# Seven-product groups in the MLP's second matrix product, strips and groups in turn, and one of four weight sums made by an accumulating DMA that GpSimd issues

## The chip, the cores and the metric

One core of one Trainium2 chip. The metric is the device time of one launch in microseconds; the median of the runs of the kernel before is 2650.49 us (three runs, 2650.14 to 2651.08).

## The reference, cut to what matters

Two transformer-like blocks run over 256 tokens of width 2048, in float32. The change lies in the MLP of the first one:

```
ff = square(relu(h @ mlp_w1 + mlp_b1))          # (256, 2048) @ (2048, 8192)
h  = layer_norm(ALPHA * h + ff @ mlp_w2 + mlp_b2)   # (256, 8192) @ (8192, 2048)
```

Ahead of it stand a mixer with recurrences and its layer norm, behind it a second block (attention, convolution, gated MLP), which the change leaves alone.

## The kernel before, in words

**Numbers in two parts.** Every float32 operand of a matmul is split into a high part (a rounded copy, made by ScalarE) and a low part (the value less its high part, made by VectorE). A product is the sum of high x high, high x low and low x high. Weights come from HBM in pieces of 128 x 1024 floats, four to a quad (q), one in each slot r of a ring of four. SP loads slot r of quad q (`quad`, L284) once the low part of quad q-1 in this slot is made; ScalarE makes the high part (`split`, L885) once the piece has landed and TensorE is through with the slot's piece of the quad before (pe_piece); VectorE makes the low part (`lo`, L1369) behind the same two conditions. TensorE waits for both (`piece_ready`, L363).

**The MLP by blocks.** `mlp` stands once on each engine (L652 TensorE, L1145 ScalarE, L1769 VectorE), for blocks i = 0 to 7 of 1024 hidden features. A block is two strips and then two pairs of output strips:
- `strip` (L370) makes 512 hidden features from `xx` with two quads, first the high (L395) then the low matmuls (L406), the first strip into the four banks of `GB` (ps_b), the second into `GA` (ps_a). At its end ScalarE copies half of the result to `half` (`halves`, L895), VectorE adds bias and both halves into `hid` (L1777, four instructions), frees the banks (strip_out), squares the positive part (L1783), and high and low parts go to `ff` (L904, L1397).
- `token_pieces` (L491) multiplies `ff`, token tile by token tile, with pieces of mlp_w2. A run is one k tile by 512 output columns; for each run and each of two token tiles t it issues three matmuls of 512 columns (L504 to L506), so 12 matmuls a piece. A pair (two output strips of 512 columns, 8 k tiles, two token tiles) is 32 products, 96 matmuls. `W2_BANKS` (L253) says which banks an output strip uses.
- VectorE adds a finished output strip from its banks to the sum `zt` in SBUF (`add_tokens`, L1755).

**Order.** The order of the work is written out by hand in each engine's program. In a block it is strip, strip, pair, pair, and each engine's waits follow from it. On VectorE the low parts of the next quads stand between the other work. While block 0's first pair runs, `turn_seed` and `keep_seed` (L642, L1141) put the residual `res` into `zt`. GpSimd has little to do: it scales `res` (L2080) before the MLP and sums squares (L2089 to L2094) in later stages. Quads 74 to 137 are the MLP's.

Of the kernel before, what the change touches and what calls it, by code (L numbers as in the profile page):

```python
# [86 lines left out]
def build(nc, x_in, prm_in, const_in, w8, w10, out):  # L87

    with ExitStack() as ctx:
# [19 lines left out]
        def in_turn(name, size, *phases):  # L109
# [4 lines left out]
        (series, _, b3), (hh,), (mx, x_res), (res, bconv, probs, probs_t, vt), (_, squares2) = in_turn(  # L114
# [4 lines left out]
            [("mx", [P, KT, 2 * S], F32R), ("x_res", [P, 2, SN, S], F32)],  # L119
            [("res", [P, KT, S], F32),  # L120
# [12 lines left out]
        (gates, aa, tt), (vv,), (zz,), (zt, stats), (bug, hsq, hnb, cqt, ckt, aqt), (x2,) = in_turn(  # L133
# [6 lines left out]
            [("zt", [P, 2, SN, 512], F32), ("stats", [P, 2, SN, 6], F32)],  # L140
# [3 lines left out]
        (uf, uu), (hid, _, rms), (bpad,), (bsq, bmean, bsdev, bpart) = in_turn(  # L144
            "region_u", 3 * SN * S,
            [("uf", [P, SN, S], F32), ("uu", [P, SN, 2 * S], F32R)],
            [("hid", [P, 2, SN, S], F32), ("gap", [P, 3 * S], F32),
# [4 lines left out]
        half = sb("half", [P, SN, S])  # L152
        prm = sb("prm", [P, NPARAM])
# [78 lines left out]
        gate_sum, gate_act = sem("gate_sum"), sem("gate_act")  # L232
        tile_done, tile_out = sem("tile_done"), sem("tile_out")
# [19 lines left out]
        W2_BANKS = (GB[:, 0:2, :], GB[:, 2:4, :], GA[:, 0:2, :], GA[:, 2:4, :])  # L253

# [28 lines left out]
        def _(sp):  # L283
# [54 lines left out]
            with sp.Fori(0, 68) as i:  # L338
                quad(i + 74, w8, 4 * i + 224, N8)
# [16 lines left out]
        def _(pe):  # L356
# [237 lines left out]
            def turn_normed(n, b):  # L594

                if b == 0:
                    pe.wait_ge(*((z_kept, 1) if n == 0 else (acc_out, 38)))
                if b == 1:
                    pe.wait_ge(*((z_kept, 5) if n == 0 else (acc_out, 40)))
# [42 lines left out]
            def turn_seed(b):  # L642
# [3 lines left out]
                for j in range(SN):  # L646
                    for t in range(2):
                        last = nc.tensor.transpose(W2_BANKS[2 + b % 2][:, t, j * P:j * P + P],
# [3 lines left out]
            def mlp(i, first=False):  # L652

                q, e = 8 * i + 74, 2 * i + E_MLP
                if first:
                    strip(q, e, GB, xx, KT, need_normed(0), free=lambda: pe.wait_ge(z_kept, 3), turns=False)
                    strip(q + 2, e + 1, GA, xx, KT, nothing)
                else:
                    strip(q, e, GB, xx, KT, nothing, free=lambda: pe.wait_ge(acc_out, 5 * i - 3), by_pairs=True)
                    strip(q + 2, e + 1, GA, xx, KT, nothing, free=lambda: pe.wait_ge(acc_out, 5 * i), by_pairs=True)  # L660
                for pair in (0, 2):
                    for c in range(2):
                        for n in (pair, pair + 1):
                            if c == 0:
                                pe.wait_ge(strip_out, outs(e + 1 + pair // 2))
                                if first and pair == 2:
                                    pe.wait_ge(seed_kept, n + 1)
                            pieces = [(q + 4 + pair + c, 2 * (n % 2) + h,
                                       [(4 * c + 2 * h, 0, 0, 512), (4 * c + 2 * h + 1, 0, 512, 512)]) for h in range(2)]
                            if n == 3 and c == 1:  # L670
                                token_pieces(pieces, W2_BANKS[n], ff, 8, need_ff(2 * i), z_half)
                                continue
                            for _, r, runs in pieces:
                                if first and pair == 0 and (c, r) in ((0, 2), (0, 3), (1, 1), (1, 2)):
                                    if (c, r) == (0, 2):
                                        pe.wait_ge(strip_out, outs(e + 2))
                                    turn_seed(((0, 2), (0, 3), (1, 1), (1, 2)).index((c, r)))
                                token_pieces([(q + 4 + pair + c, r, runs)], W2_BANKS[n], ff, 8, need_ff(2 * i))

            mlp(0, True)  # L680
            with pe.Fori(0, 7) as i:
                mlp(i + 1)

            pe.wait_ge(acc_out, 37)
# [20 lines left out]
            strip(138, E_IN2, GB, xx, KT, need_normed(1), free=lambda: pe.wait_ge(acc_out, 37), turns=False)  # L705
# [178 lines left out]
        def _(act):  # L884
# [256 lines left out]
            def keep_seed(b):  # L1141
                act.wait_ge(seed_turned, b + 1)
                act.activation(zt[:, :, b, :], W2_BANKS[2 + b % 2], ACT.Copy).then_inc(seed_kept, 1)

            def mlp(i, first=False, last=False):  # L1145
                q, e = 8 * i + 74, 2 * i + E_MLP
                for k in range(2):
                    if not (first and k == 0):
                        splits(q + 2 * k + 1)
                    splits(q + 2 * k + 2)  # L1150
                    halves(e + k, 4 * (q + 2 * k) + 8, psum[1 - k])
                    hi_of(ff[:, 4 * k:4 * k + 4, 0:S], hid[:, k, :, :], ff_made, 2 * i + k + 1, ff_hi)
                if first:
                    splits(q + 5, N8, (0, 1))
                    keep_seed(0)
                    split(q + 5, 2)
                    keep_seed(1)
                    split(q + 5, 3)
                    split(q + 6, 0)
                    keep_seed(2)  # L1160
                    split(q + 6, 1)
                    keep_seed(3)
                    splits(q + 6, N8, (2, 3))
                else:
                    splits(q + 5)
                    splits(q + 6)
                if last:
                    act.activation(warm[:, 1:2], eps[:, 0:1], ACT.Sqrt)
                splits(q + 7)
                splits(q + 8, N8, (0, 1) if last else range(RING))  # L1170

            mlp(0, True)
            with act.Fori(0, 6) as i:
                mlp(i + 1)
            mlp(7, last=True)
# [190 lines left out]
        def _(dve):  # L1366
# [388 lines left out]
            def add_tokens(i, q, n, t, count):  # L1755

                if isinstance(i, int) and i == 0:
                    dve.wait_ge(seed_kept, n + 1)
                else:
                    dve.wait_ge(acc_out, 5 * i - 4 + count)  # L1760
                if t == 0:
                    dve.wait_ge(z_half, i + 2)
                else:
                    dve.wait_ge(pe_piece, 4 * (q + 5 + n - n % 2) + 2 + 2 * (n % 2))
                blocks = slice(0, 2) if t is None else t
                dve.tensor_tensor(zt[:, blocks, n, :], W2_BANKS[n][:, blocks, :], zt[:, blocks, n, :], ALU.add
                                  ).then_inc(acc_out, 1)

            def mlp(i, first=False, last=False):  # L1769
                q, e = 8 * i + 74, 2 * i + E_MLP  # L1770
                for k in range(2):
                    if not (first and k == 0):
                        los(q + 2 * k + 1)
                    los(q + 2 * k + 2, N8, (0, 1, 2))
                    dve.wait_ge(half_out, e + k + 1)
                    for j in range(SN):
                        ins = dve.scalar_tensor_tensor(hid[:, k, j, :], psum[1 - k][:, j, 0:S],  # L1777
                                                       column("b1", 4 * k + j + 8 * i), half[:, j, :], ALU.add, ALU.add)
                    ins.then_inc(strip_out, 1)
                    lo(q + 2 * k + 2, 3)  # L1780
                    dve.wait_ge(strip_out, outs(e + k + 1))

                    dve.scalar_tensor_tensor(hid[:, k, :, :], hid[:, k, :, :], 0.0, hid[:, k, :, :], ALU.max,  # L1783
                                             ALU.mult).then_inc(ff_made, 1)
                    lo_of(ff[:, 4 * k:4 * k + 4, S:2 * S], hid[:, k, :, :], ff[:, 4 * k:4 * k + 4, 0:S],
                          2 * i + k + 1, ff_hi, ff_lo)

                def summed(n):
                    if last:
                        dve.wait_ge(acc_out, 36 + n)  # L1790
                        for t in range(2):
                            strip_stats(n, t, zt[:, t, n, :])

                los(q + 5)
# [416 lines left out]
```

## Time and profile before

| | us |
|---|---|
| median of three runs | 2650.49 |
| lowest, highest | 2650.14, 2651.08 |
| span of the profiled execution, first to last instruction | 2647.7 |
| TensorE busy | 2631.6 (99%) |
| VectorE busy | 1745.8 (66%) |
| ScalarE busy | 1362.4 (51%) |
| GpSimd busy | 36.1 (1%) |

The page gives the profiled execution's span; its own whole time is not printed apart from the three runs' times. A row of a timeline is a start, a length, the engine and what it did; "x4" says that four like instructions are merged in it, and brackets give the idle time ahead and what ended it. Consecutive instructions of one engine overlap a little: the length of one is a bit more than the distance of two starts. A matmul's length holds its way through the array; the pace is the distance of the starts. PE is TensorE, PEld its weight loads, DVE VectorE, ACT ScalarE, POOL GpSimd, SP the engine that issues the loads.

### The profile page before, as it was taken

How to read it: one execution, taken by the hardware profiler on the slowest of the kernel's cores; microseconds unless marked ns; L12 is line 12 of the kernel's file. 1: busy time of each engine (PE TensorE's matmuls, PEld its weight loads, DVE VectorE, ACT ScalarE, POOL GpSimd, SP SyncE). 2: the span in 40 equal slices, each digit the busy share in tenths (PEclk: the TensorE clock that was granted, in tenths of full speed). 3: DMA queues.
4: the chain of work that ended last, by engine and by line, in shares of the span. 5: the costliest groups of instructions: out<-in, count | busy, mean ns of one | idle time of the engine just before them, and what ended most of it. 6: DMA issues, size and time to landing. Idle time of an engine off the chain costs nothing.

```text
span 2647.7 us, 40522 instructions
## 1 busy us (share of the span) xinstructions
PE 2631.6 (99%) x14379; PEld 2279.8 (86%) x14379; DVE 1745.8 (66%) x1863; ACT 1362.4 (51%) x1588; POOL 36.1 (1%) x30
## 2 busy tenths in 40 slices
PE   9999999999999999999999999999999999999999
PEld 8888888888888888888888888878888888888888
DVE  7787877544455655555555568996666666666667
ACT  5767765444444544444444445587554444444444
POOL 0000000000000100000000001000100000000000
PEclk9999999999999999999999999999999999999999
DMA  7555555555656455556555664534555555555554
GB/s 266 181 186 184 191 186 195 197 182 189 201 198 199 160 187 193 176 192 202 192 178 193 198 195 153 177 129 147 171 191 190 188 186 188 190 190 190 190 190 168
DMA packets 133881, 494.01 MB, mean 187 GB/s; under 512 B 14864, under 2 KB 15376, under 8 KB 133776
## 3 DMA queue, kind: packets, MB, share of 16 engines
q1 hardware_dynamic: 133776, 492.62, 56.4%
q8 instruction: 65, 1.06, 0.2%
q14 instruction: 40, 0.33, 0.0%
HBM read 490.46 MB, written 2.10 MB: 186 GB/s over the span
## 4 chain that ended last, share of the span: by engine, by line
PE 92%; DVE 3%; ACT 2%; issue 2%; DMA 0%; DVEq 0%; SPq 0%; ACTq 0%
PE ps_b L395 18%; PE ps_a L395 18%; PE ps_b L406 10%; PE ps_a L406 10%; PE ps_b L504 6%; PE ps_b L506 6%; PE ps_b L505 6%; PE ps_a L505 5%; PE ps_a L504 5%; PE ps_a L506 5%; DVE w_lo L1373 1%; PE ps_b L826 1%; ACT w_hi L889 1%; DVE bconv L1874 1%; DVE gates L1519 1%
## 5 line engine op out<-in xcount | busy, mean ns | idle before, releaser
L1373 DVE TENSOR_TENSOR w_lo<-w_raw,w_hi 128x1024 fp32r<-128x1024 f32 (+1 forms) x908 | 1120.4, 1251 | 726.3 <-ACT w_hi L889 716.9
L889 ACT ACTIVATE w_hi<-w_raw 128x1024 fp32r<-128x1024 f32 (+1 forms) x908 | 966.9, 1075 | 1105.1 <-PE ps_a L506 237.1
L395 PE MATMUL ps_b<-xx,w_hi 128*128 128x512 f32 x1184 | 287.9, 392 | 4.0 <-DVE xx L1690 2.3
L395 PE MATMUL ps_a<-xx,w_hi 128*128 128x512 f32 x1120 | 269.1, 391 | 0.0
L395 PEld LDWEIGHTS ps_b<-xx,w_hi 128*128 128x128 f32 x1184 | 216.9, 188 | 47.7 <-ACT w_hi L889 3.7
L395 PEld LDWEIGHTS ps_a<-xx,w_hi 128*128 128x128 f32 x1120 | 205.8, 188 | 39.8
L395 PE MATMUL ps_a<-x,w_hi 128*128 128x512 f32 x704 | 165.9, 390 | 0.0
L395 PE MATMUL ps_b<-x,w_hi 128*128 128x512 f32 x704 | 165.5, 390 | 0.0
L406 PEld LDWEIGHTS ps_b<-xx,w_lo 128*128 128x128 f32 x1184 | 153.2, 192 | 5.8
L406 PE MATMUL ps_b<-xx,w_lo 128*128 128x256 f32 x1184 | 156.0, 284 | 0.0
L395 PEld LDWEIGHTS ps_b<-x,w_hi 128*128 128x128 f32 x704 | 130.8, 188 | 26.2
L395 PEld LDWEIGHTS ps_a<-x,w_hi 128*128 128x128 f32 x704 | 130.6, 188 | 26.1
L406 PEld LDWEIGHTS ps_a<-xx,w_lo 128*128 128x128 f32 x1120 | 142.3, 191 | 4.4
L406 PE MATMUL ps_a<-xx,w_lo 128*128 128x256 f32 x1120 | 144.4, 283 | 0.0
L504 PE MATMUL ps_b<-w_hi,xx 128*128 128x512 f32 (+1 forms) x320 | 122.6, 383 | 0.0
L506 PE MATMUL ps_b<-w_hi,xx 128*128 128x512 f32 (+1 forms) x320 | 121.3, 379 | 0.0
L505 PE MATMUL ps_b<-w_lo,xx 128*128 128x512 f32 (+1 forms) x320 | 121.3, 379 | 0.0
L504 PE MATMUL ps_b<-w_hi,ff 128*128 128x512 f32 x256 | 99.9, 390 | 0.0
L506 PE MATMUL ps_b<-w_hi,ff 128*128 128x512 f32 x256 | 99.6, 389 | 0.0
L505 PE MATMUL ps_b<-w_lo,ff 128*128 128x512 f32 x256 | 99.6, 389 | 0.0
L504 PE MATMUL ps_a<-w_hi,ff 128*128 128x512 f32 x256 | 99.6, 389 | 0.0
L505 PE MATMUL ps_a<-w_lo,ff 128*128 128x512 f32 x256 | 99.6, 389 | 0.0
(305 smaller groups left out, 3933.5 us busy)
## 6 DMA issues: line engine op xcount, KB each, us to landing
w_raw<-w_dram SPq DMA_DIRECT2D x836, 512.0 KB, 3.4
w_raw<-w_dram SPq DMA_DIRECT2D x72, 640.0 KB, 3.9
zz<-x_dram SPq DMA_DIRECT2D x8, 256.0 KB, 4.6
x_res<-x_dram SPq DMA_DIRECT2D x4, 512.0 KB, 6.0
out_dram<-res SPq DMA_DIRECT2D x3, 512.0 KB, 2.8
out_dram<-res SPq DMA_DIRECT2D x4, 128.0 KB, 2.1
const<-const_dram SPq DMA_DIRECT2D x1, 449.0 KB, 4.5
prm<-prm_dram SPq DMA_DIRECT2D x1, 308.0 KB, 5.4
```

What stands on the lines that cost most here:

```text
L395: last = nc.tensor.matmul(group[:, j, :], w_hi[:, r, o * P:o * P + P], moving(src, at + k), start=begins and k == 0, stop=not begins and k ...
L406: last = nc.tensor.matmul(group[:, j, 0:S], w_lo[:, r, o * P:o * P + P], moving(src, at + k)[:, 0:S], start=begins and k == 0, stop=not be ...
L504: nc.tensor.matmul(dst, x_hi, hi, start=k == 0 and not begun, stop=False)
L505: nc.tensor.matmul(dst, x_hi, lo, start=False, stop=False)
L506: last = nc.tensor.matmul(dst, x_lo, hi, start=False, stop=k == kt - 1)
L826: nc.tensor.matmul(banks[:, j // 2, (j % 2) * S:(j % 2) * S + S], w_hi[:, r, cols], mix_tile(k)[:, half_at:half_at + S], start=False, stop ...
L889: act.activation(w_hi[:, r, 0:width], w_raw[:, r, 0:width], ACT.Copy).then_inc(hi_done, 1)
L1373: dve.tensor_tensor(w_lo[:, r, 0:width], w_raw[:, r, 0:width], w_hi[:, r, 0:width].bitcast(F32), ALU.subtract).then_inc(lo_even if r % 2 = ...
L1519: own.done(dve.tensor_tensor_scan(gates[:, hd, way, 0, order], aa[:, way, hd, order], tt[:, way, hd, order], 0.0, ALU.mult, ALU.add))
L1874: ins = dve.scalar_tensor_tensor(y, x, column("cv_w", n), y, ALU.mult, ALU.add)
```

## The change

Blocks are taken apart and put in turn: strip, pair, strip, pair. All strips but the second use `GB`. The strip of a block's first half is made ahead of the second pair of the block before. In 13 of the 16 pairs (block 0's second, both of blocks 1 to 6) the 2 x 2 x 2 products of two token tiles, two k tiles and two output strips on k tiles 2 and 3, and again on 4 and 5, are made by seven products instead of eight (Winograd's form); k tiles 0, 1, 6 and 7 stay as they were. The seven need sums of inputs and of weights:
- four sums of `ff` tiles (`next_inputs_of`), once a block on VectorE, with their high and low parts in spare columns of the ring (`s_hi_of`, `s_lo_of`);
- four sums of weights. The one for m5 is made in the ring slot by a DMA from HBM that adds the other piece to what has landed (`added`, GpSimd), the other three by two VectorE subtractions from it (`mixed_pieces`). These three get high and low parts of 1536 columns (`t_high`, `t_low`); ScalarE and VectorE take the slot's own parts only after the DMA has landed (t1_in).
- Four of the products go to the four banks of `GB`, and VectorE adds them into `q_acc` in SBUF (two adds a pair, `group_end`), three with the plain products into `GA`, added to `zt` as before. `q_acc` is cleared by GpSimd and combined into `zt` by `combined`, five VectorE instructions for each of the two pairs, in and after block 6.

The last block writes to `ff_last` and runs in the old order of banks. SP's order of pieces within a grouped pair changes with it (`by_groups`).

```diff
+        def product_operands(g, wh, wl, r0, buf):
...
+            return dict(m1=(GB[:, 0, :], tile(k, 0), piece(r0, 0)),
+                        m2=(GA[:, 0, :], tile(k + 1, 0), piece(r0, 1)),
+                        m3=(GA[:, 2, :], summed(3), piece(r1, 1)),
+                        m4=(GA[:, 1, :], tile(k + 1, 1), mixed_piece(2)),
+                        m5=(GB[:, 1, :], summed(0), piece(r1, 0)),
+                        m6=(GB[:, 2, :], summed(1), mixed_piece(0)),
+                        m7=(GB[:, 3, :], summed(2), mixed_piece(1)))
...
+            def seven_products(i, g, done, q, r0):
+
+                m = product_operands(g, w_hi, w_lo, r0, g)
+                piece_ready(q, r0)
+                product(m["m1"], g == 0, g == 1)
+                product(m["m2"], False, False).then_inc(pe_piece, 1)
+                piece_ready(q, r0 + 1)
+                product(m["m5"], g == 0, g == 1)
+                product(m["m3"], False, False).then_inc(pe_piece, 1)
+                pe.wait_ge(t_hi, done + g + 1)
+                pe.wait_ge(t_lo, done + g + 1)
+                product(m["m6"], g == 0, g == 1)
+                last = product(m["m7"], g == 0, g == 1)
+                if g == 1:
+                    last.then_inc(q_out, 1)
+                product(m["m4"], False, False).then_inc(t_used, 1)
+
+            def grouped(i, pair, q):
...
+                for nn in range(2):
+                    pe.wait_ge(acc_out, 2 * n - 1 + nn)
+                    token_pieces([(q, nn, two_tiles(0))], sums_of(nn), ff, 8, need)
...
+                seven_products(i, 0, 2 * n - 2, q, 2)
+                need(4)
+                seven_products(i, 1, 2 * n - 2, q + 1, 0)
+                for nn in range(2):
+                    token_pieces([(q + 1, 2 + nn, two_tiles(6))], sums_of(nn), ff, 8, nothing)
...
+            def mlp(i):
+
+                q, e = 8 * i + 80, E_MLP + 2 * i + 3
+                grouped(i, 0, q)
+                up_strip(q + 2, e, lambda: pe.wait_ge(q_kept, 4 * i))
+                grouped(i, 1, q + 4)
...
+            def second_of(n, q, r0):
+
+                act.wait_ge(t1_in[1 - r0 // 2], 8 * n + 16 - 8 * (1 - r0 // 2))
+                split(q, r0 + 1)
...
+            def strip_end(q, e, k, sums, n):
+
+                splits(q + 2, N8, (0, 1, 2))
+                if sums is not None:
+                    act.wait_ge(s_lo, sums + 1)
+                halves(e, 4 * q + 8, GB)
+                second_of(n, q + 2, 2)
+                t_high(n, 0)
+
+            def group_end(q, n):
+
+                split_group(n + 1, q + 1, 0)
+                t_high(n + 1, 1)
+                splits(q + 1, N8, (2, 3))
+                splits(q + 2)
...
+            def mixed_pieces(n, q, r0, buf):
+
+                even, odd = w_raw[:, r0, 0:N8], w_raw[:, r0 + 1, 0:N8]
+                made = t_raw[:, buf, :]
+                dve.wait_ge(raw_in[r0], 16 * q + 16)
...
+                dve.wait_ge(t1_in[buf], 8 * n + 16 - 8 * buf)
+                own.done(dve.tensor_tensor(made[:, 0:512], odd[:, 0:512], odd[:, 512:N8], ALU.subtract))
+                own.need()
+                dve.tensor_tensor(made[:, 512:1536].rearrange("p (h c) -> p h c", h=2),
+                                  even.rearrange("p (h c) -> p h c", h=2),
+                                  made[:, 0:512].unsqueeze(1).to_broadcast([P, 2, 512]), ALU.subtract).then_inc(t_made, 1)
...
+            def strip_end(q, i, k, n):
+
+                e = E_MLP + 2 * i + k
+                los(q + 2, N8, (0, 1))
+                activated(e, i, k, GB)
+                squared(e + 1, k)
+                mixed_pieces(n, q + 2, 2, 0)
+                los(q + 2, N8, (2, 3))
+                t_low(n, 0)
+
+            def group_end(q, pair, n, done):
+
+                mixed_pieces(n + 1, q + 1, 0, 1)
+                los(q + 1, N8, (0, 1))
+                t_low(n + 1, 1)
+                los(q + 1, N8, (2, 3))
+                los(q + 2, N8, (0, 1))
+                dve.wait_ge(q_out, done + 1)
+                for h in range(2):
+                    dve.tensor_tensor(q_acc[:, pair, 2 * h:2 * h + 2, :], GB[:, 2 * h:2 * h + 2, :],
+                                      q_acc[:, pair, 2 * h:2 * h + 2, :], ALU.add).then_inc(q_kept, 1)
+                lo(q + 2, 2)
+                add_sums(pair, 0, 4 * q + 7)
+                lo(q + 2, 3)
+                add_sums(pair, 1, 4 * q + 8)
...
+            pool.wait_ge(seed_kept, 4)
+            pool.memset(q_acc[:, :, :, :], 0.0).then_inc(q_zero, 1)
+
+            def added(n, q, at, r0):
+
+                pool.wait_ge(raw_in[r0 + 1], 16 * q + 16)
+                pool.dma_start(w_raw[:, r0 + 1, 0:512], w8[ds(at, 1), :, 0:512].rearrange("a p n -> (a p) n"),
+                               accum_op=ALU.add).then_inc(t1_in[1 - r0 // 2], 16)
```

## Rows read from the trace of the kernel before

**Rows 1.** The page: engines' busy time, and the chain that ended last, by engine.
```profile
PE 2631.6 (99%) x14379; PEld 2279.8 (86%) x14379; DVE 1745.8 (66%) x1863; ACT 1362.4 (51%) x1588; POOL 36.1 (1%) x30
PE 92%; DVE 3%; ACT 2%; issue 2%; DMA 0%; DVEq 0%; SPq 0%; ACTq 0%
```

**Rows 2.** Busy time by windows, one MLP block: us, engines, granted clock, DMA share, GB/s.
```profile
1245.30:1333.40 88.10, 88.10 (x450) 75.53 (x449) 50.88 (x50) 37.05 (x36) 0.00 (x0) 1.00 0.58 191
```

**Rows 3.** Timeline of TensorE: two strips and the first pair of that block.
```profile
1245.30 3.79 PE L395 MATMUL ps_b<-xx,w_hi 128*128 128x512 f32 x16
...
1267.53 3.79 PE L395 MATMUL ps_a<-xx,w_hi 128*128 128x512 f32 x16
...
1289.76 0.39 PE L504 MATMUL ps_b<-w_hi,ff 128*128 128x512 f32 x1
...
1311.52 0.39 PE L504 MATMUL ps_a<-w_hi,ff 128*128 128x512 f32 x1
```

**Rows 4.** Groups of VectorE by line and form: busy us, mean ns, idle before.
```profile
L1373 DVE TENSOR_TENSOR w_lo<-w_raw,w_hi 128x1024 fp32r<-128x1024 f32 x836 | 1014.4, 1231 | 659.1 <-ACT w_hi L889 651.6 <-DVE hid L1385 3.4 <-DVE padded L1385 1.9
L1373 DVE TENSOR_TENSOR w_lo<-w_raw,w_hi 128x1280 fp32r<-128x1280 f32 x72 | 106.1, 1490 | 67.2 <-ACT w_hi L889 65.3 <-issue 1.7
...
L1842 DVE TENSOR_TENSOR hid<-hid,rms 128x1024 f32<-128x1024 f32 x22 | 26.8, 1219 | 0.0
...
L1766 DVE TENSOR_TENSOR zt<-ps_b,zt 128x1024 f32<-128x1024 f32 x16 | 19.6, 1224 | 6.7 <-PE ps_b L506 6.7
...
L1397 DVE TENSOR_TENSOR xx<-zz,xx 128x512 fp32r<-128x512 f32 x8 | 5.5, 686 | 2.6 <-ACT xx L908 2.6
```

**Rows 5.** Groups of ScalarE by line and form.
```profile
L889 ACT ACTIVATE w_hi<-w_raw 128x1024 fp32r<-128x1024 f32 x836 | 875.1, 1058 | 1006.9 <-PE ps_b L506 221.7 <-PE ps_a L506 184.1 <-PE ps_b L395 173.2
L889 ACT ACTIVATE w_hi<-w_raw 128x1280 fp32r<-128x1280 f32 x72 | 91.7, 1274 | 98.2 <-PE ps_a L506 52.9 <-PE ps_a L448 11.1 <-PE ps_b L448 9.3
```

**Rows 6.** Timelines of ScalarE and of VectorE behind the strip's end at 1267.53.
```profile
1267.79 1.06 ACT L889 ACTIVATE w_hi<-w_raw 128x1024 fp32r<-128x1024 f32 x1 [0.81 <-PE ps_b L395]
1268.75 1.01 ACT L900 ACTIVATE half<-ps_b 128x1024 f32<-128x1024 f32 x1
...
1269.90 1.66 DVE L1777 SCALAR_TENSOR_TENSOR hid<-ps_b,prm,half 128x256 f32<-128x256 f32 x4 [1.58 <-ACT half L900]
...
1276.10 3.50 DVE L1373 TENSOR_TENSOR w_lo<-w_raw,w_hi 128x1024 fp32r<-128x1024 f32 x3
```

**Rows 7.** Timelines: VectorE behind a wait on itself, TensorE behind one on VectorE.
```profile
1807.14 0.69 DVE L1938 TENSOR_TENSOR bpart<-bconv 128x512 f32<-128x512 f32 x1
1807.87 0.42 DVE L1940 TENSOR_TENSOR bpart<-bpart 128x256 f32<-128x256 f32 x1
...
1820.36 0.42 DVE L1940 TENSOR_TENSOR bpart<-bpart 128x256 f32<-128x256 f32 x1
...
1820.93 0.67 PE L626 MATMUL ps_a<-bpart,ones 128*128 128x256 f32 x2 [0.72 <-DVE bpart L1940]
```

**Rows 8.** The page: DMA issues, KB each, us from issue to landing.
```profile
w_raw<-w_dram SPq DMA_DIRECT2D x836, 512.0 KB, 3.4
...
zz<-x_dram SPq DMA_DIRECT2D x8, 256.0 KB, 4.6
...
out_dram<-res SPq DMA_DIRECT2D x4, 128.0 KB, 2.1
```

**Rows 9.** Timelines of GpSimd and VectorE where both work, in order of time.
```profile
903.34 3.69 DVE L1373 TENSOR_TENSOR w_lo<-w_raw,w_hi 128x1024 fp32r<-128x1024 f32 x3
903.52 12.24 POOL L2080 TENSOR_SCALAR res<-res,prm 128x256 f32<-128x256 f32 x16 [903.08 <-DVE xx L1687]
...
1625.71 9.59 POOL L2089 TENSOR_TENSOR squares<-squares 128x1024 f32<-128x1024 f32 x3 [709.95 <-ACT squares L1126]
1626.72 6.31 DVE L1373 TENSOR_TENSOR w_lo<-w_raw,w_hi 128x1024 fp32r<-128x1024 f32 x2 [0.38 <-ACT w_hi L889]
...
1874.33 2.61 POOL L2089 TENSOR_TENSOR squares<-squares 128x1024 f32<-128x1024 f32 x1 [235.08 <-ACT squares L1126]
```

**Rows 10.** Busy time by windows, where TensorE stands still now and then (columns as rows 2).
```profile
1820.00:1840.00 20.00, 18.11 (x156) 16.67 (x155) 13.74 (x21) 17.08 (x37) 0.00 (x0) 1.00 0.38 125
```

More of the change, by code:

```diff
@@ L647, in turn_seed @@
                     for t in range(2):
-                        last = nc.tensor.transpose(W2_BANKS[2 + b % 2][:, t, j * P:j * P + P],
+                        last = nc.tensor.transpose(W2_BANKS[b % 2][:, t, j * P:j * P + P],
                                                    res[:, SN * b + j, t * P:t * P + P], ident)
                 last.then_inc(seed_turned, 1)
[L652 to L678, printed above, removed]
@@ L680, in _, with two_tiles, up_strip, product @@
-            mlp(0, True)
-            with pe.Fori(0, 7) as i:
-                mlp(i + 1)
-            pe.wait_ge(acc_out, 37)
+            def two_tiles(k):
+                return [(k, 0, 0, 512), (k + 1, 0, 512, 512)]
+            def up_strip(q, e, free):
+                strip(q, e, GB, xx, KT, nothing, free=free, by_pairs=True)
+            def product(operands, begins, ends):
+                bank, (a_hi, a_lo), (b_hi, b_lo) = operands
+                nc.tensor.matmul(bank, a_hi, b_hi, start=begins, stop=False)
+                nc.tensor.matmul(bank, a_hi, b_lo, start=False, stop=False)
+                return nc.tensor.matmul(bank, a_lo, b_hi, start=False, stop=ends)
@@ new lines, in in_order @@
+            def in_order(q, banks, src, need, begin=None, beside=None, apart=None):
+                for c in range(2):
+                    for nn in range(2):
+                        if c == 0 and begin is not None:
+                            begin(nn)
+                        pieces = [(q + c, 2 * nn + h, two_tiles(4 * c + 2 * h)) for h in range(2)]
+                        if apart is not None and (c, nn) == (1, 1):
+                            token_pieces(pieces, banks(nn), src, 8, need, apart)
+                            continue
+                        for _, r, runs in pieces:
+                            if beside is not None:
+                                beside(c, r)
+                            token_pieces([(q + c, r, runs)], banks(nn), src, 8, need)
@@ L1753, in _, with add_tokens @@
             first_blocks(0, 74)
[L1755 to L1764, printed above, removed]
+            def add_tokens(n, banks, t, count):
@@ new lines, in next_inputs_of @@
+            def next_inputs_of(i, q):
+                dve.wait_ge(ff_made, 2 * i + 2)
+                h = pairs[:, 1:3, :, :, :]
+                one, two, three_, four = (s_sum[:, n, :, :] for n in range(4))
+                own.done(dve.tensor_tensor(one, h[:, :, 0, 1, :], h[:, :, 1, 1, :], ALU.add))
+                own.need()
+                own.done(dve.tensor_tensor(two, one, h[:, :, 0, 0, :], ALU.subtract))
+                own.need()
+                own.done(dve.tensor_tensor(three_, h[:, :, 0, 1, :], h[:, :, 0, 0, :], ALU.subtract))
+                dve.tensor_tensor(four, h[:, :, 1, 0, :], two, ALU.subtract).then_inc(s_made, 1)
+                ff_low(ff, i, 0)
+                lo(q + 1, 0)
+                ff_low(ff, i, 1)
+                lo(q + 1, 1)
+                lo_of(s_lo_of, half[:, :, :], s_hi_of, i + 1, s_hi, s_lo)
+                los(q + 1, N8, (2, 3))
```

350 lines of the change are left out of this document (258 added, 92 removed).

## The prediction, made before the changed kernel was run

> **What bounds the kernel now.** I read the page first: TensorE is busy 99% of the span, VectorE 66%, ScalarE 51%, GpSimd 1%, and the chain that ended last lies 92% on TensorE [rows 1]. Then one block of the MLP by windows: from 1245.30 to 1333.40 TensorE is busy for all 88.10 us, at full granted clock (2.4 GHz), VectorE 50.88 us and ScalarE 37.05 us [rows 2]. So the stage is matmul after matmul, and only fewer matmuls could shorten it, as long as the others keep up. Last the timelines, for the pace: a strip starts at 1245.30 and the next at 1267.53, so a strip costs 22.23 us; the 96 token products of a pair of output strips start at 1289.76 and the next pair at 1311.52, 21.76 us or 0.2267 us a matmul [rows 3]. A token piece of 12 matmuls is 2.72 us.
>
> **What the change removes.** In 13 groups (block 0's second pair, both pairs of blocks 1 to 6) the 16 products on k tiles 2 to 5 become 14. A product is three matmuls, so a pair falls from 96 matmuls to 90, 20.40 us, 1.36 us less. 13 x 1.36 = **-17.7 us**.
>
> **What it adds.** On TensorE nothing. On VectorE, per block of two strips and two pairs: four 512-wide subtractions (0.69 each), four 1024-wide ones with a broadcast input (1.22, the price of the broadcast product of L1842), four low parts of 1536 (1.75: 1.231 at 1024, 1.490 at 1280, so 0.26 more for 256 more), four more PSUM adds (1.22), and once four 256-wide sums (0.46, with a wait) and a low part (1.23) [rows 4, 7]. That is 2.8 + 4.9 + 7.0 + 4.9 + 1.8 + 1.2 = 22.6 us more on 50.9, so 73.5 of some 85 us. VectorE is not the bound by its total. What matters is where the work stands, because a ring slot is prepared only four pieces ahead. ScalarE gets four high parts of 1536 (1.49: 1.058 at 1024, 1.274 at 1280) and one of 1024 [rows 5], 7 us in all on 37; not a bound.
>
> **The walk through one group.** Count from E, the end of the strip ahead (E = 1267.53 in the block shown). TensorE's own course would be: plain pieces 0 and 1 of quad q until 5.44; products on slot 2 until 6.80, on slot 3 until 8.16, the three that need the mixed pieces until 10.20; the same for quad q+1 until 14.96; two plain pieces until 20.40. VectorE's course begins with the strip's end, which in the new order is always directly ahead of a group:
> - ScalarE is released 0.26 after E (1267.79) and VectorE starts on the strip 1.15 after the copy of the half (1268.75 to 1269.90) [rows 6]. The copy now goes ahead of the split of slot 3, so it starts at E+0.26 and VectorE at E+1.41.
> - Four additions take 1.66, until 3.07. A wait of VectorE on itself costs 0.04 (1807.14 + 0.69 to 1807.87) [rows 7]. The square starts at 3.11; without a wait the next instruction starts 1.14 later ((3.50 - 1.23)/2) [rows 6], at 4.25.
> - Mixed pieces: 0.69 + 0.04, then 1.22: ends 6.20. Slots 2 and 3 may be taken low only now (lows free the raw slots): 6.12 to 7.35, 7.26 to 8.49. ScalarE's high part of the mixed pieces runs beside, 6.23 to 7.72. The low part runs 8.40 to 10.15.
> - TensorE wanted slot 2 at 5.44. A wait of TensorE on VectorE ends 0.15 after the instruction (1820.36 + 0.42 to 1820.93) [rows 7], so it goes on at 7.50, is through slots 2 and 3 at 10.22, waits for the low part until 10.30 and ends the first seven at 12.34: 2.14 late.
> - Second seven: mixed pieces 10.06 to 12.01, lows of slots 0 and 1 until 13.16 and 14.30, low part of the mixed pieces 14.21 to 15.96. TensorE waits for slot 0 until 13.31, is at the mixed products at 16.03, gets them at 16.11, ends them at 18.15: **3.19 late**. The plain pieces at the end have their lows at 17.10 and 18.24, before they are due (18.15, 20.87).
>
> So from E+1.41 to E+15.96 VectorE has no gap, and TensorE needs that chain done at 12.77 (its own course to the mixed products of the second seven, 12.92, less 0.15). The stalls start afresh in each group, since the chain hangs on the strip's end. The group ends at 23.59 where 21.76 was before: +1.83, and 13 x 1.83 = **+23.8 us**.
>
> **What else is moved.** After a group VectorE takes two lows (until 20.4), the two adds out of the B banks (until 22.8, 0.8 before TensorE wants these banks for the next strip), two more lows and the two sums, until 3.7 after the group's end. In strips where the next inputs are made it is then busy until about 14.6 of the strip, while the strip's low matmuls on its second quad come at 14.8 to 17.6: covered, with 0.1 to 3 us to spare, and if that cover goes the strip waits by the excess. At the end combined(1) puts 5.2 us and a low part 1.2 us ahead of the lows of quad 135: these end at 11.4 where TensorE wants them at 10.9, **+0.6 us** with the release. The strips alternate through the B banks alone; their adds are out in time as said, so nothing for that. SP's ring loads are freed by the lows: the latest (slot 3, next-inputs strip) is issued at E-7.6.
>
> **The accumulating DMA** has no row. It waits for the raw piece: an issue at E-7.6 with 3.4 us to landing [rows 8] gives E-4.2 (elsewhere E-5.1). VectorE wants the sum at 4.25, so 8.45 us are free; the second one has from E+0.6 to 10.06, 9.4 us. Ends: 2.1 us (a 128 KB transfer) and 9.2 us (twice the 4.6 of a 256 KB load, since the destination is read as well) [rows 8]. At 9.2 it is 0.75 us late, x 13 = +9.8 us. I take nothing, from the single 4.6 us load, the nearest in size. Queued behind it: on ScalarE the split of slot 3 and then the high part of the mixed pieces, on VectorE the whole chain, on GpSimd the next issue; its sums of squares, first at 1625.71 [rows 9], come long after. By the Trainium skill, "DMA: Bandwidth & Descriptors", section on the anatomy of one DMA, such a transfer costs 2.0 us and bytes/436e3, an estimate of 2.6 us here, which adds nothing to the sum; no run here shows it.
>
> GpSimd is not idle to its neighbours: while it ran tensor_tensor at 1625.71, two lows took 6.31 us instead of 2.36; while it ran tensor_scalar at 903.52, three lows took 3.69, nearly their usual 3.50 [rows 9]. Issuing a transfer lies between: 0 to 2.0 us a piece. The first falls into a VectorE gap, the second about E+0.7, beside the four additions. I take 0, as for tensor_scalar, since the issue has no second operand; the upper end, half a microsecond a group on average, is +6.5 us.
>
> **Sum:** -17.7 + 13 x 3.19 (41.5) + 0.6 = +24.4. On the profiled span, 2647.7 to 2672.1. The page gives that execution's span only; the three whole times, 2650.14 to 2651.08, lie 2.4 to 3.4 us above it. On the median: 2650.5 + 24.4 = **2675 us**.
>
> **Rivals.**
> - The chain is covered, and the fewer products show: this needs the lateness below 1.36 us a group, that is VectorE's 14.5 us chain shorter by 1.83. Place: the ten SBUF-to-SBUF subtractions of the two halves, 11.8 us of the chain; if they ran in under 85% of their rows' time in the new shapes (broadcast, 1536 wide, the sum in place) it would turn. Fully covered it gives 2650.5 - 17.7 = 2633. Against it: widths 512, 1024, 1280 and a broadcast all lie on one line of about 1 ns an element [rows 4]. Chance 0.10.
> - The accumulating DMA is late. Beyond 8.45 us every microsecond adds 13 us. At 12 us: 3.55 late behind next-inputs strips, 2.65 behind the others, some 40 us, 2715. For it: an issue by GpSimd, of which the trace has none, a destination that is read too, and GpSimd's access to SBUF that VectorE's lows can hold up (at 1625.71 three of its 1024-wide operations took 9.59, a single one at 1874.33 took 2.61) [rows 9]. Against it: 8.45 us is far over all rows but the bound. Chance 0.14. The page "SBUF — State Buffer", section on who interferes with whom, of the Trainium skill says that descriptor writing is held up by two-port VectorE modes and not (inferred) by tensor_tensor; by that the transfer is in time.
> - Other small shortages in the same direction (port, strips with 0.1 us of cover) are in the range, not a case.
> - Both effects cancel within 0.2% (5.3 us, about what a measurement can tell from no change): lateness of 0.95 to 1.8 us a group. Chance 0.03.
> - The clock falls in the gaps: at 1820 to 1840 TensorE stood still for 1.9 of 20 us at full granted clock [rows 10]; here it would be 3.2 of 46. No chance of its own.
>
> **Numbers.** Forecast as walked 0.73, late transfer 0.14, covered 0.10, cancelled 0.03: faster 0.10, same 0.03, slower 0.87. Range: below, 1 us a group less lateness (13 us) to 2661; above, 9.8 + 6.5 + some strip waits to 2698. Outside lie the covered case and most of the late transfer.
>
> **What would show it.** In the profile after: 78 fewer matmuls (13 x 6), TensorE waiting on w_lo L1373 near E+5.4 (about 1.9 us) and E+12.3 (1 us) and hardly on the mixed low part (0.1), 13 times each; VectorE near 100% from E+1.4 to E+16; strips still 22.2 us; clock 1.00; the accumulate landing before E+4. If ScalarE or VectorE waits there for the DMA, the second rival holds; if TensorE has no gaps, the first.

## The result, and the profile after

The changed kernel takes 2680.98 us in the median of four runs (2680.42 to 2684.34) against 2650.31 for the kernel before: 30.7 us more. The ratio over all runs is 1.0119, with a 95% interval of 1.0104 to 1.0133. The forecast was 2675 in a range of 2661 to 2698. The profiled execution is the slowest of the four, 2684.34 us with a span of 2682.3; 2.2 us of its length lie ahead of the MLP, in work that the change leaves alone (the first strip behind the layer norm starts at 889.95 instead of 887.73).

The page of the changed kernel, parts 1, 4 and 6, which answer to [rows 1, 8]:

```profile
span 2682.3 us, 40396 instructions
PE 2634.6 (98%) x14301; PEld 2268.3 (85%) x14301; DVE 1886.6 (70%) x2005; ACT 1405.4 (52%) x1621; POOL 62.1 (2%) x57
...
PE 83%; DVE 7%; issue 4%; ACT 3%; DMA 2%; DVEq 0%; SPq 0%; ACTq 0%; POOLq 0%
...
w_raw<-w_dram POOLq DMA_DIRECT2D x26, 256.0 KB, 4.5
```

The 78 matmuls are gone (14379 to 14301), and yet the end is later: VectorE's share of the chain rose from 3% to 7%. The timelines of one group (block 3, second pair) say why. The strip ahead ends at 1284.59, the next one starts at 1308.83. First TensorE, with two rows of the group behind it, then VectorE:

```profile
1284.59 0.39 PE L574 MATMUL ps_a<-w_hi,ff 128*128 128x512 f32 x1
...
1289.80 0.39 PE L576 MATMUL ps_a<-w_hi,ff 128*128 128x512 f32 x1
1292.12 0.67 PE L731 MATMUL ps_b<-w_hi,ff 128*128 128x512 f32 x1 [1.93 <-DVE w_lo L1557]
1292.59 0.63 PE L732 MATMUL ps_b<-w_lo,ff 128*128 128x512 f32 x1
...
1308.83 3.79 PE L465 MATMUL ps_b<-xx,w_hi 128*128 128x512 f32 x16
...
1338.50 0.50 PE L731 MATMUL ps_b<-w_hi,ff 128*128 128x512 f32 x1 [1.84 <-DVE w_lo L1557]
1344.30 0.50 PE L731 MATMUL ps_b<-w_hi,ff 128*128 128x512 f32 x1 [0.62 <-DVE w_lo L1557]
...
1286.06 1.66 DVE L1971 SCALAR_TENSOR_TENSOR hid<-ps_b,prm,half 128x256 f32<-128x256 f32 x4 [4.27 <-ACT half L1029]
1287.75 1.23 DVE L1977 SCALAR_TENSOR_TENSOR hid<-hid 128x1024 f32<-128x1024 f32 x1
1288.98 0.69 DVE L1958 TENSOR_TENSOR t_raw<-w_raw 128x512 f32<-128x512 f32 x1
1289.71 1.23 DVE L1960 TENSOR_TENSOR t_raw<-w_raw,t_raw 128x1024 f32<-128x1024 f32 x1
1290.85 2.35 DVE L1557 TENSOR_TENSOR w_lo<-w_raw,w_hi 128x1024 fp32r<-128x1024 f32 x2
1293.12 1.76 DVE L1581 TENSOR_TENSOR tlo<-t_raw,thi 128x1536 fp32r<-128x1536 f32 x1
1294.79 0.69 DVE L1958 TENSOR_TENSOR t_raw<-w_raw 128x512 f32<-128x512 f32 x1
1295.51 1.22 DVE L1960 TENSOR_TENSOR t_raw<-w_raw,t_raw 128x1024 f32<-128x1024 f32 x1
1296.65 2.35 DVE L1557 TENSOR_TENSOR w_lo<-w_raw,w_hi 128x1024 fp32r<-128x1024 f32 x2
1298.92 1.75 DVE L1581 TENSOR_TENSOR tlo<-t_raw,thi 128x1536 fp32r<-128x1536 f32 x1
```

VectorE sits idle for 4.27 us, from 2.80 us ahead of the strip's end to 1.47 us behind it, and then works from 1286.06 to 1300.67 with no gap. TensorE stands at 1290.0 and gets slot 2 at 1292.12. In the next group (the rows at 1338.50 and 1344.30, strip's end at 1331.05) it stands twice, until 7.45 and 13.25 us of the group. The first wait is there in all 13 groups, the second in eight of them.

Where the time went, from TensorE's timeline: between the MLP's first strip and the strip behind the next layer norm lie 746.96 us (889.95 to 1636.91), before 714.85 (887.73 to 1602.58), 32.1 more. The 13 groups take 312.9 us together instead of 13 x 21.76 = 282.9, 30.0 more; the 13 strips between them 289.9 instead of 289.0; the last block with the layer norm 50.07 instead of 48.90 (the wait for quad 135, 0.89 of it).

The granted clock moves too. By windows of the changed kernel (columns as [rows 2]): the first matmuls behind the standstill, their group, and the strip ahead:

```profile
1292.12:1295.50 3.38, 3.38 (x8) 2.72 (x9) 3.35 (x3) 2.33 (x3) 0.00 (x0) 0.52 0.85 224
1284.59:1308.83 24.24, 22.31 (x92) 17.98 (x90) 22.29 (x22) 12.14 (x11) 0.86 (x1) 0.93 0.65 200
1262.25:1284.59 22.34, 22.34 (x130) 19.74 (x129) 11.52 (x10) 8.29 (x8) 0.86 (x1) 1.00 0.60 191
```

For some 3.4 us it is granted 1.2 instead of 2.4 GHz, a matmul each 0.43 us. This happened in six of the 13 groups, always behind the first wait.

One more wait stands at the end of some groups. VectorE's adds out of the B banks were to end at 22.8 us of the group. In the one that starts at 1331.05 they end at 23.96, and the next strip wants these banks:

```profile
1352.66 2.35 DVE L2003 TENSOR_TENSOR q_acc<-ps_b,q_acc 128x1024 f32<-128x1024 f32 x2
1355.15 3.91 PE L465 MATMUL ps_b<-xx,w_hi 128*128 128x512 f32 x16 [0.19 <-DVE q_acc L2003]
```

Behind five of the 13 groups the strip starts 0.17 to 0.35 us late, each time just after such adds end, 1.2 us in all.

### The profile page after: what moved, and what is told of

Its sections match the earlier page's. It is cut to its first block, busy times and chain, and to the rows that moved or that the text cites. A ratio compares the mean times of both kernels' runs of the same rounds, so it can differ in the third digit from the quotient of the medians.

```text
span 2682.3 us, 40396 instructions
## 1 busy us (share of the span) xinstructions
PE 2634.6 (98%) x14301; PEld 2268.3 (85%) x14301; DVE 1886.6 (70%) x2005; ACT 1405.4 (52%) x1621; POOL 62.1 (2%) x57
## 4 chain that ended last, share of the span: by engine, by line
PE 83%; DVE 7%; issue 4%; ACT 3%; DMA 2%; DVEq 0%; SPq 0%; ACTq 0%; POOLq 0%
PE ps_b L465 20%; PE ps_a L465 14%; PE ps_b L476 10%; PE ps_a L476 7%; PE ps_a L574 4%; PE ps_a L575 4%; PE ps_a L576 4%; PE ps_b L574 4%; PE ps_b L576 4%; PE ps_b L575 4%; DVE w_lo L1557 3%; DMA w_raw<-w_dram 2%; ACT w_hi L1018 1%; PE ps_b L955 1%; PE ps_b L731 1%
## 5 line engine op out<-in xcount | busy, mean ns | idle before, releaser
L465 PE MATMUL ps_b<-xx,w_hi 128*128 128x512 f32 x1632 | 394.3, 392 | 4.9 <-DVE xx L1874 2.3
L465 PEld LDWEIGHTS ps_b<-xx,w_hi 128*128 128x128 f32 x1632 | 299.6, 188 | 67.6 <-issue 4.9
L476 PEld LDWEIGHTS ps_b<-xx,w_lo 128*128 128x128 f32 x1632 | 208.8, 192 | 6.9
L476 PE MATMUL ps_b<-xx,w_lo 128*128 128x256 f32 x1632 | 211.9, 283 | 0.0
L465 PE MATMUL ps_a<-xx,w_hi 128*128 128x512 f32 x672 | 163.8, 391 | 0.0
L465 PEld LDWEIGHTS ps_a<-xx,w_hi 128*128 128x128 f32 x672 | 122.6, 188 | 23.2
L574 PE MATMUL ps_a<-w_hi,ff 128*128 128x512 f32 x240 | 93.7, 391 | 0.0
L576 PE MATMUL ps_a<-w_hi,ff 128*128 128x512 f32 x240 | 93.4, 389 | 0.0
L476 PEld LDWEIGHTS ps_a<-xx,w_lo 128*128 128x128 f32 x672 | 86.7, 191 | 4.8 <-DVE w_lo L1557 1.4
L476 PEld LDWEIGHTS ps_a<-x,w_lo 128*128 128x128 f32 x704 | 87.8, 192 | 1.9
L476 PEld LDWEIGHTS ps_b<-x,w_lo 128*128 128x128 f32 x704 | 87.4, 192 | 1.7
```

Source lines behind the costliest of these rows:

```text
L465: last = nc.tensor.matmul(group[:, j, :], w_hi[:, r, o * P:o * P + P], moving(src, at + k), start=begins and k == 0, stop=not begins and k ...
L476: last = nc.tensor.matmul(group[:, j, 0:S], w_lo[:, r, o * P:o * P + P], moving(src, at + k)[:, 0:S], start=begins and k == 0, stop=not be ...
L574: nc.tensor.matmul(dst, x_hi, hi, start=k == 0 and not begun, stop=False)
L576: last = nc.tensor.matmul(dst, x_lo, hi, start=False, stop=k == kt - 1)
```

## The experiments

Group lengths are read in TensorE's timeline, from the first token matmul behind a strip to the first matmul of the next strip; the mean is over the first 12 groups.

| kernel | median us | ratio to before, 95% | mean group us |
|---|---|---|---|
| before (a pair) | 2649.4 to 2650.5 | | 21.76 |
| changed | 2680.98 | 1.0104 to 1.0133 | 24.12 |
| filled_gap | 2681.40 | 1.0107 to 1.0141 | 23.86 |
| no_fourth_sum | 2681.54 | 1.0103 to 1.0137 | 23.92 |
| sum_on_vector | 2697.67 | 1.0166 to 1.0200 | 25.31 |
| order_alone | 2653.82 | 1.0003 to 1.0022 | 22.03 |
| square_late | 2679.77 | 1.0102 to 1.0133 | 23.23 |
| square_late_no_sum | 2668.47 | 1.0058 to 1.0089 | 22.51 |
| early_vector_sum | 2635.02 | 0.9936 to 0.9963 | 20.41 |
| early_dma_sum | 2696.39 | 1.0153 to 1.0184 | 25.25 |
| early_square_in_place | 2647.95 | 0.9984 to 1.0003 | 21.65 |
| early_combined_late | 2634.61 | 0.9926 to 0.9953 | 20.42 |

**A longer chain: sum_on_vector.**

```diff
-                dve.wait_ge(t1_in[buf], 8 * n + 16 - 8 * buf)
+                dve.wait_ge(raw_in[r0 + 1], 16 * q + 16)
+                dve.tensor_tensor(odd[:, 0:512], odd[:, 0:512], even[:, 0:512], ALU.add).then_inc(t1_in[buf], 16)
+                dve.wait_ge(t1_in[buf], 8 * n + 16 - 8 * buf)
```

and `added` goes from GpSimd.

> The fourth weight sum goes from the accumulating DMA to VectorE, a 512-wide addition with a wait, 0.73 us, ahead of each half of a group. If TensorE waits for VectorE's chain behind the strip's end, both waits grow, by 1.46 us a group and 19 us in all: 2700 (2694 to 2704 as the clock falls or not). If it was the accumulating DMA that came late, taking it away gains at least 0.4 us a group: 2675 or less.

2697.67, 16.7 us more than the changed kernel; TensorE's first wait ends at 8.18 instead of 7.45 us of the group, the second at 14.71 instead of 13.25: 0.73 and 1.46 later, as the additions are long. So the chain sets the time.

**No accumulating DMA: no_fourth_sum.**

```diff
-                dve.wait_ge(t1_in[buf], 8 * n + 16 - 8 * buf)
+                dve.wait_ge(raw_in[r0 + 1], 16 * q + 16)
...
-                act.wait_ge(t1_in[1 - r0 // 2], 8 * n + 16 - 8 * (1 - r0 // 2))
```

`added` goes from GpSimd here too, so the fourth sum is left out.

> The accumulating DMA is left out and nobody makes the fourth weight sum, so the weights of m5 and the mixed pieces lack a term. If VectorE's chain alone counts, the DMA was just in time and the time stays at 2681 within 2 us, with the same wait of 1.85 us at 7.45 us of a group. If the DMA holds ScalarE's split or VectorE's subtraction back, the time falls by 5 us or more.

2681.54: the median doesn't move, and the waits end at 7.45 and 13.25 still. In the changed kernel the DMA costs nothing that the medians show. In the profile it comes late in one of the 13 groups, the one that starts at 1052.48:

```profile
1057.07 0.69 DVE L1958 TENSOR_TENSOR t_raw<-w_raw 128x512 f32<-128x512 f32 x1 [0.36 <-DMA w_raw<-w_dram]
```

There TensorE's first wait ends at 7.73 instead of 7.45.

**The order without the seven products: order_alone.** `grouped` becomes `in_order(q, sums_of, ff, need_ff(2 * i), begin=...)`, SP loads the quads in their old order, VectorE's sums, mixed pieces and adds into `q_acc` and GpSimd's DMAs go, and `squared` stays directly behind `activated`.

> Strips and pairs in turn as in the changed kernel, the last block with its own ff_last, but all products the plain ones: no sums, no seven products, no accumulating DMA, 96 matmuls a pair. If the cost lies in the groups of seven alone, each pair takes 21.8 us again with TensorE never waiting, and the time is that of the kernel before, 2650.5 within 2 us. If the new order itself costs something at strip ends, it stays above 2655.

2653.82, some 3.3 to 4.2 us above before, so neither answer quite. Its TensorE timeline, one group that starts at 1226.44:

```profile
1231.65 0.39 PE L576 MATMUL ps_a<-w_hi,ff 128*128 128x512 f32 x1
1232.03 0.50 PE L574 MATMUL ps_a<-w_hi,ff 128*128 128x512 f32 x1
1232.36 0.39 PE L575 MATMUL ps_a<-w_lo,ff 128*128 128x512 f32 x1
1232.59 0.40 PE L576 MATMUL ps_a<-w_hi,ff 128*128 128x512 f32 x1
```

Where starts lie 0.23 apart otherwise, they lie 0.38 and 0.33 apart: slot 2's low part stands behind the additions and the square even here and comes 0.15 us late, and the matmul that had to wait costs 0.11 more. A pair is 0.27 longer, 13 to 14 times. That is some 3.5 us for the new order; the other 27 come with the seven products.

**The clock: filled_gap.**

```diff
+                keep_busy(8, GB[:, 0, :])
                 seven_products(i, 0, 2 * n - 2, q, 2)
```

> Eight matmuls on a zero operand stand where TensorE waits about 1.9 us behind each strip; they change no result. If six of the 13 groups are longer (24.4 us against 23.9) because the granted clock fell after that standstill, all 13 come out near 23.8 us at full granted clock and the time falls by some 3 to 5 us, to 2676 to 2678. If the clock is not the cause and only VectorE's chain counts, nothing changes: 2681 within 1 us. The eight matmuls take 1.81 us, so they should not lengthen the wait.

By windows of this kernel, two groups:

```profile
1281.33:1305.04 23.71, 23.01 (x99) 17.95 (x98) 21.50 (x22) 12.05 (x11) 0.86 (x1) 1.00 0.61 191
1235.35:1259.10 23.75, 23.04 (x99) 18.11 (x98) 21.74 (x22) 12.05 (x11) 0.86 (x1) 1.00 0.67 192
```

The clock stays at full in every group and the profiled groups are shorter, 23.86 against 24.12, but the median is 2681.40: no gain, a miss. Five of the six groups at 1.2 GHz have no second wait (at 1284.59 there is none, at 1331.05 there is), since a TensorE that works slowly meets VectorE's chain at the same point; what it loses it would mostly have stood. The runs' mean granted clock points the same way: the changed kernel took 2680.54 us at 0.996 and 2681.43 and 2680.42 at 0.998, filled_gap 2680.24 to 2684.08 at 0.999 each time. Three microseconds in one profiled execution against none in the medians, whose runs spread over 3.8 us, stay unsettled.

**A shorter chain: square_late, square_late_no_sum.**

```diff
                 activated(e, i, k, GB)
-                squared(e + 1, k)
                 mixed_pieces(n, q + 2, 2, 0)
...
                 add_sums(pair, 1, 4 * q + 8)
+                squared(E_MLP + 2 * i + k + 1, k)
```

With it the parts of the last block's first half (`ff_high`, `ff_low` of `ff_last`) go behind block 6's first group. square_late_no_sum is the same without the DMA and without the fourth sum.

> The squaring of a finished strip (1.14 us of VectorE's path) goes from directly behind the additions to the end of the group. If the chain counts by its length alone, both waits of TensorE shrink, the group falls from 24.1 to about 22.5 us (0.84 and 0.97 us of waiting instead of 1.85 and 0.6, and no fall of the clock), and the time to 2660 (2657 to 2664). If the accumulating DMA, which landed about 3.7 to 4.3 us behind the strip's end, is next in line, VectorE waits for it from 3.0 on, only part is gained, and the time is 2664 to 2674.

> square_late without the accumulating DMA; the fourth weight sum is left out. Both theories give the chain's own time here, 2660 (2657 to 2664); the difference to square_late is what the DMA costs once the chain is shorter: nothing if only the chain counts, 4 to 14 us if the DMA is next in line.

2679.77 and 2668.47. Both are above all their ranges, two misses. Their difference, 11.3 us, is in the range forecast for a DMA that is next in line. In square_late_no_sum the waits end at 6.18 and 11.98, 1.27 earlier each, as long as the square takes on VectorE's path (1287.72 to 1288.98 in the changed kernel). VectorE's timeline of square_late, a strip's end at 1277.35:

```profile
1278.83 1.66 DVE L1971 SCALAR_TENSOR_TENSOR hid<-ps_b,prm,half 128x256 f32<-128x256 f32 x4 [4.27 <-ACT half L1029]
1281.39 0.69 DVE L1958 TENSOR_TENSOR t_raw<-w_raw 128x512 f32<-128x512 f32 x1 [0.91 <-DMA w_raw<-w_dram]
```

The subtraction now waits 0.91 us for the DMA. The groups vary from 22.3 to 25.2 us with it and from 22.2 to 22.7 without, where 22.5 was expected: by groups, the theory holds. What both expectations left out is the end. The square of the last strip had moved ahead of quad 135's low parts as well, and TensorE waits 2.6 and 3.2 us there (0.89 in the changed kernel). In square_late_no_sum the layer norm comes 4.3 us later against the last group: 2.3 us are the longer wait, and behind it the granted clock fell for 3.4 us, at a place where TensorE does not wait again:

```profile
1579.64:1583.05 3.41, 3.41 (x10) 2.64 (x9) 2.46 (x3) 0.00 (x0) 0.00 (x0) 0.50 0.86 241
```

The miss there was 8.5 us by the median. The profiled execution (2665.53, granted clock 0.999) is the fastest of the four; the others, at 0.997 and 0.998, took 1.7 to 4.3 us more, and where is not shown.

**VectorE's idle time used: early_vector_sum.** The fourth sum as in sum_on_vector, and

```diff
                 los(q + 2, N8, (0, 1))
-                activated(e, i, k, GB)
-                squared(e + 1, k)
                 mixed_pieces(n, q + 2, 2, 0)
-                los(q + 2, N8, (2, 3))
+                lo(q + 2, 2)
+                activated(e, i, k, GB)
+                lo(q + 2, 3)
                 t_low(n, 0)
...
                 t_low(n + 1, 1)
+                squared(E_MLP + 2 * i + k + 1, k)
                 los(q + 1, N8, (2, 3))
-                los(q + 2, N8, (0, 1))
                 dve.wait_ge(q_out, done + 1)
...
-                lo(q + 2, 2)
+                los(q + 2, N8, (0, 1, 2))
```

The low part of the input sums goes behind quad q+1's in `next_inputs_of`, and the split of the last block's first half behind block 6's first group.

> The fourth sum is made by VectorE, and it, the mixed pieces and the low part of slot 2 go ahead of the strip's end, where VectorE stood idle for 4.3 us; the squaring goes behind the group's last mixed low part, the adds out of the B banks ahead of the next quad's lows. By the chain theory the mixed low parts are then ready at about 5.8 and 12.5 us of the group, where TensorE wants them at 8.2 and 12.9: no waits, a group of 20.4 us, and the time 2650.5 - 17.7 + 1 to 2 for the end, 2634 (2632 to 2639). If the loads land later than the 5 us after their issue that the trace shows, VectorE reaches the strip's end late and the time is 2640 or more. If the alternation or the seven products cost something else, not the chain, it stays above 2650.

2635.02, as expected, 14.4 us below the kernel before and faster than both kernels. VectorE's timeline, a strip's end at 1261.07:

```profile
1258.20 0.68 DVE L1958 TENSOR_TENSOR w_raw<-w_raw 128x512 f32<-128x512 f32 x1
1258.91 0.69 DVE L1960 TENSOR_TENSOR t_raw<-w_raw 128x512 f32<-128x512 f32 x1
1259.64 1.23 DVE L1962 TENSOR_TENSOR t_raw<-w_raw,t_raw 128x1024 f32<-128x1024 f32 x1
...
1262.56 1.66 DVE L1973 SCALAR_TENSOR_TENSOR hid<-ps_b,prm,half 128x256 f32<-128x256 f32 x4 [0.56 <-ACT half L1029]
...
1265.26 1.75 DVE L1581 TENSOR_TENSOR tlo<-t_raw,thi 128x1536 fp32r<-128x1536 f32 x1
...
1271.79 1.75 DVE L1581 TENSOR_TENSOR tlo<-t_raw,thi 128x1536 fp32r<-128x1536 f32 x1
```

The idle 4.27 us before the strip's additions are 0.56. The mixed low parts are ready at 5.94 and 12.47 us of the group, before 8.2 and 12.9, and by windows two strips and two groups (1218.41 to 1303.70) are pure matmul again, with VectorE busy for 73.17 of the 85.29 us (the third engine of the columns):

```profile
1218.41:1303.70 85.29, 85.29 (x437) 73.13 (x436) 73.17 (x74) 43.28 (x41) 0.00 (x0) 1.00 0.61 197
```

**The same order with the DMA: early_dma_sum.** Only the fourth sum differs from early_vector_sum.

> The order of early_vector_sum (2635.0), but with the fourth sum left to the accumulating DMA as in the changed kernel. It landed 3.7 to 4.3 us behind the strip's end there, and VectorE now waits for it ahead of the strip's own additions. If the DMA's landing is what a shorter chain runs into, the additions end near 8.7 instead of 4.8, TensorE gets slot 2 about 3.4 us late and the second half another 0.9, a group of 24.7, and the time is 2690 (2675 to 2700). If only the order counts, it is 2632 to 2640.

2696.39. In the group that starts at 1287.95 VectorE's and TensorE's timelines have

```profile
1292.08 0.69 DVE L1958 TENSOR_TENSOR t_raw<-w_raw 128x512 f32<-128x512 f32 x1 [6.93 <-DMA w_raw<-w_dram]
...
1296.96 0.60 PE L731 MATMUL ps_b<-w_hi,ff 128*128 128x512 f32 x1 [3.41 <-DVE hid L1971]
```

VectorE stands 6.93 us for the DMA, with the strip's additions queued behind it, and TensorE 3.41 us for them. GpSimd issued the DMA at 1284.50; VectorE went on 7.6 us later. Two of the first 12 groups, with landings 1.3 and 1.9 us behind the strip's end, stayed near 23 us.

**The square in its old place: early_square_in_place.**

```diff
                 activated(e, i, k, GB)
+                squared(e + 1, k)
                 lo(q + 2, 3)
...
-                squared(E_MLP + 2 * i + k + 1, k)
```

The parts of the last block's first half are back ahead of block 6's first group as well.

> early_vector_sum with the squaring back directly behind the strip's additions. By the chain the first half still has cover (mixed low part at 7.1 us, wanted at 8.2), the second has not: slot 0's low part ends at 10.8 where TensorE wants it at 10.2, with its restart 0.75 us a group, and one low part of the last block's inputs more in block 6. 2645 (2641 to 2648). If the squaring lies in a gap anyway, 2635.

2647.95, 12.9 us above early_vector_sum. TensorE's only wait ends at 10.98 us of the group (expected 10.8), and 11 of the first 12 groups take 21.3 to 21.5. The one of block 6 with the extra low part takes 24.10, so 3.7 of the 12.9 us lie there and not all of them are the square's: its wait ends 1.23 later than the others', and the clock falls behind it.

**The last combination later: early_combined_late.** `combined(1)` goes from before `los(135)` to behind `summed(1)`.

> early_vector_sum with the last combination of the sums (5.2 us of VectorE) moved behind the second output strip of the last block, where VectorE has gaps. TensorE's waits in the last block, 0.30 and 1.08 us there, go: 2633.6, that is 1 to 2 us below early_vector_sum, which the medians may not resolve and the profile should. If the gaps are too small, the layer norm behind starts later and the time is 2635 or more.

2634.61, which the medians don't tell from 2635.02. In the profile the last group and the last block take 70.49 instead of 71.46 us; the wait of 1.08 is gone. The first one (0.30, and 0.44 here) stays: it lies in the last group, not in the last block.

## Why the prediction was right, and where its terms were off

**The mechanism** stood as walked: a fixed chain on VectorE that hangs on the strip's end, longer than the gain of 1.36 us a group. Its end was put at 15.96 us of the group and measured at 16.08 (1300.67 - 1284.59); TensorE was to go on at 7.50 and 13.31 and did at 7.45 and 13.25. The experiments with a chain 0.73 us longer for each half, and with the square out of it, moved TensorE's waits by these lengths. The gain was real too: early_vector_sum has it in its groups, 20.41 where 20.40 was computed. Of 17.7 us it shows 14.4 in the medians; the last group and block take 71.46 instead of 20.40 + 48.91, 2.2 of the difference.

Three of the signs that were named did not come: the second wait stood in eight groups and not in 13, the clock did not stay at 1.00, and three accumulating DMAs landed later than 4 us behind the strip's end.

**The size**: +24.4 forecast, +30.7 measured. The term that was too small is 13 x 1.83 = 23.8; the 13 groups measure 30.0, 2.31 each. The difference of 6.2 us has these parts, read in the profile:
- A wait was priced at 0.15 us for the release and nothing for the restart. The release takes 0.04 (slot 2's low part ends at 1292.08, the matmul starts at 1292.12) and the restart 0.11 (0.50 instead of 0.39 at 1338.50), which is the same for one wait; but the last wait, a few hundredths long, was priced at 0.08 and costs 0.16. With it, groups without a fall of the clock are 23.5 to 24.1 long where 23.59 was computed.
- In block 6 `ff_low(ff_last, 7, 0)` stands inside the chain, ahead of the second half's mixed pieces: the walk missed it, and that group takes 24.87, some 1.1 more.
- The adds out of the B banks were given 0.8 us to spare and end too late in five groups, 1.2 us.
- The late DMA of one group, 0.3 us.
- Some 2 us, an estimate against the groups without a fall, lie in the other five groups in which the clock fell, and there filled_gap leaves the cause open, as said.

**The accumulating DMA** was put at nothing, and it costs nothing that the medians show, but that was luck. The walk gave it 8.45 us and 4.6 for the transfer. It began later and took longer. At 1323.19 VectorE's last low part frees slot 3, the load of this slot is issued at 1323.36 and lands 4.5 us later instead of 3.4, and GpSimd issues 0.65 behind that, at 1328.48: 2.6 us ahead of the strip's end, not 4.2. Over the 13 groups the first DMA took 5.3 to 7.8 us and landed 1.2 to 4.5 behind the strip's end, where VectorE wants it at 4.39 (1288.98 in the group shown). One was late by 0.36, one landed just in time: no margin, which no_fourth_sum alone would not have shown. The second DMA of a group took 3.6 to 3.8 us each time. Two rows of GpSimd's timeline, each with the time to landing behind it:

```profile
1289.75 0.86 POOL L2391 DMA_DIRECT2D w_raw<-w_dram  x1 [7.76 <-DMA w_raw<-w_dram]
w_raw<-w_dram POOLq DMA_DIRECT2D x1, 256.0 KB, 3.6
...
1328.48 0.86 POOL L2391 DMA_DIRECT2D w_raw<-w_dram  x1 [37.86 <-DMA w_raw<-w_dram]
w_raw<-w_dram POOLq DMA_DIRECT2D x1, 256.0 KB, 6.2
```

The slow ones ran beside two of SP's ring loads; beside the fast ones no such load was under way or issued in the first 2.4 us. That the loads slow it is read from this pattern of 13 and 13 and was not tested by itself. The fit of the Trainium skill, "DMA: Bandwidth & Descriptors", section on the anatomy of one DMA, gives an estimate of 2.6 us for this size. The trace does not agree: 3.6 us at the least. The late-transfer rival is no rival in the changed kernel and the cause in square_late and early_dma_sum.

**GpSimd beside VectorE** was rightly put at nothing: the issue at 1289.75 lies on VectorE's 1024-wide subtraction at 1289.71, which took 1.23 us as anywhere. The Trainium skill, "SBUF — State Buffer", section on who interferes with whom, holds (as an inference) that tensor_tensor does not hold up descriptor writing. The trace agrees: the DMA issued beside that subtraction landed in 3.6 us, while the one at 1328.48 was issued with VectorE idle (1328.26 to 1332.53) and took 6.2.

**The end** was put at 0.6 and is 1.2. **The clock** was forecast to stay up, from a stretch with 1.9 us of standstill in 20: that was wrong, it fell in six groups. What that costs in time stayed below what the medians tell.

## What to carry to other kernels

A saving on the engine that bounds a kernel is worth only what its helpers can follow at that point: with the same work on VectorE, sum_on_vector takes 2697.67 us and early_vector_sum 2635.02, by placement alone, and VectorE's share of the span is no warning of it (70% in the changed kernel, 72% in early_vector_sum). Look for where the helper was idle just ahead of a chain (4.27 us here), put the work that doesn't depend on the event there, and put work nobody waits for (the square) behind the chain. A transfer taken from an engine's path must be judged by its landing against the new, shorter path, and never stand in front of work that others wait for.

## What the runs showed of the hardware beyond what was expected

- The accumulating DMA of 256 KB by GpSimd landed 3.6 to 3.8 us after its issue where no ring load was under way or issued in its first 2.4 us, and 5.3 to 7.8 beside two of them; the issue itself takes GpSimd 0.86 us. The median of 4.5 on the page mixes the two.
- A wait of TensorE on a late operand, even of 0.15 us or less, costs 0.08 to 0.11 us more in the matmul behind it.
- Standstills of about 1.9 us each 46 us let the granted clock fall from 2.4 to 1.2 GHz for 3.4 us in six of 13 groups, and in no_fourth_sum, with the same standstills, in four. With eight matmuls on zeros in the gap it stayed at 2.4 GHz, and the median did not move.
- A fall of the clock cost some 0.4 us in the groups of the changed kernel, where TensorE would have waited again. At the end of square_late_no_sum, where it doesn't, it costs about 1.7 us, an estimate: 3.4 us with a matmul each 0.43 us instead of 0.227.
